# Four attentions of a two-block fp32 kernel: the maximum of a group of heads is taken ahead of the scaling of the group before

## What is computed

```python
logits = einsum(q_i, k_t) * scale + d_i - d_k        # first block, causal
p = softmax(where(mask, logits, MASK_VALUE)); o = einsum(p, v_t)

p = softmax(einsum(qb, k)); o = einsum(p, v)         # second block, "A" (axial) and "C" (latent)
p = softmax(sc); p = p[:, :, 0] - lam * p[:, :, 1]   # second block, "B" (differential)
```

## Time and profile before

| what | us |
|---|---|
| median of 3 runs (2878.01 to 2881.4) | 2878.91 |
| the profiled execution, its own time | 2877.92 |
| its span, first to last instruction | 2876.1 |
| PE busy / PE weight loads | 2621.8 / 2333.3 |
| DVE busy / ACT busy | 1857.5 / 1528.5 |
| mean granted TensorE clock, share of full | 0.947 |

### The profile page before, as it was taken

The page is one execution under the profiler, slowest core; times in us unless marked ns, Lnnn a source line. Parts: engine busy times, 40 slices in busy tenths (PEclk is TensorE's granted clock), DMA queues, the critical chain, the costliest instruction groups (busy, mean ns, idle before and its releaser), DMA issues.

```text
span 2876.1 us, 38647 instructions
## 1 busy us (share of the span) xinstructions
PE 2621.8 (91%) x16826; PEld 2333.3 (81%) x16826; DVE 1857.5 (65%) x1580; ACT 1528.5 (53%) x1466; POOL 0.2 (0%) x4
## 2 busy tenths in 40 slices
PE   6879999887999999999999997978799989878998
PEld 6769998776787877878787786877689988768998
DVE  5645445564688888888888884454565554546554
ACT  5244434432677767777776774455344444644443
POOL 0000000000000000000000000000000000000000
PEclk9879999987999999999999998999899999889999
DMA  5214554221599999989999894323145533223452
GB/s 202 90 58 147 183 185 158 100 79 59 193 366 349 365 350 361 354 348 362 348 365 351 349 364 158 118 88 132 54 152 191 189 134 118 82 95 114 151 191 88
DMA packets 83099, 585.32 MB, mean 204 GB/s; under 512 B 9480, under 2 KB 11208, under 8 KB 12272
## 3 DMA queue, kind: packets, MB, share of 16 engines
q1 hardware_dynamic: 82928, 582.81, 54.2%
HBM read 581.73 MB, written 1.05 MB: 203 GB/s over the span
## 4 chain that ended last, share of the span: by engine, by line
PE 82%; DVE 10%; ACT 6%; issue 1%; DMA 0%; ACTq 0%; SPq 0%; DVEq 0%
PE PS L1370 80%; ACT whi L500 2%; DVE wlo L842 2%; ACT pb L563 2%; PE PS L1754 1%; ACT pt L579 1%; PE PS L1516 1%; DVE hT L859 1%; DVE stat L937 1%; DVE pb L945 1%; DVE small L855 1%; DVE hT L910 0%; DVE pb L931 0%; DVE qe L1003 0%; DVE ke L1002 0%
## 5 line engine op out<-in xcount | busy, mean ns | idle before, releaser
L842 DVE TENSOR_TENSOR wlo<-raw,whi 128x2048 fp32r<-128x2048 f32 x550 | 1259.5, 2291 | 567.2 <-ACT whi L500 557.1
L500 ACT ACTIVATE whi<-raw 128x2048 fp32r<-128x2048 f32 x550 | 1052.0, 1913 | 375.4 <-PE PS L1370 375.3
L1370 PE MATMUL PS<-hhi,whi 128*128 128x256 f32 x1952 | 573.1, 294 | 31.9 <-DVE hlo L865 19.0
L1370 PE MATMUL PS<-hlo,whi 128*128 128x256 f32 x1952 | 563.9, 289 | 0.0
L1370 PE MATMUL PS<-hhi,wlo 128*128 128x256 f32 x1952 | 562.9, 288 | 0.0
L1370 PEld LDWEIGHTS PS<-hhi,whi 128*128 128x128 f32 x1952 | 385.7, 198 | 46.5 <-issue 40.6
L1370 PEld LDWEIGHTS PS<-hlo,whi 128*128 128x128 f32 x1952 | 386.6, 198 | 0.6 <-issue 0.5
L1370 PEld LDWEIGHTS PS<-hhi,wlo 128*128 128x128 f32 x1952 | 385.7, 198 | 0.0
L1370 PE MATMUL PS<-whi,xghi 128*128 128x512 f32 x896 | 360.0, 402 | 2.1 <-ACT pm L667 2.1
L1370 PE MATMUL PS<-whi,xglo 128*128 128x512 f32 x896 | 355.2, 396 | 0.0
L1370 PE MATMUL PS<-wlo,xghi 128*128 128x512 f32 x896 | 355.0, 396 | 0.0
(11 more groups left out here) (331 smaller groups left out, 3757.3 us busy)
## 6 DMA issues: line engine op xcount, KB each, us to landing
raw<-in_wm SPq DMA_DIRECT2D x336, 1024.0 KB, 5.0
raw<-in_ws SPq DMA_DIRECT2D x214, 1024.0 KB, 4.8
xT<-in_xT SPq DMA_DIRECT2D x1, 1024.0 KB, 4.9
bsum<-in_bsum SPq DMA_DIRECT2D x1, 1024.0 KB
out_T<-hT SPq DMA_DIRECT2D x4, 256.0 KB, 2.5
lmask<-in_lmask SPq DMA_DIRECT2D x1, 512.0 KB
tri<-in_tri SPq DMA_DIRECT2D x1, 256.0 KB
cmask<-in_cmask SPq DMA_DIRECT2D x1, 256.0 KB
```

Source lines behind the costliest of these rows:

```text
L500: act.activation(whi[s % SPLIT][:], raw[s % RAW][:], ACT.Copy).then_inc(hi_ready, 1)
L842: dve.tensor_tensor(wlo[s % SPLIT][:], raw[s % RAW][:], whi[s % SPLIT][:].bitcast(F32), ALU.subtract).then_inc(lo_ready, 1)
L1370: return pe.matmul(out, a, b, start=start, stop=stop, skip_group_check=True)
```

## The change

In each of the three `attention` functions the index of the later steps moves by one, and the loop runs one n longer. On DVE the scaling of group n-1 now follows the maximum of group n; the transpose is of group n-2 and the value product of group n-3. No buffer, bank, instruction or size changes. Because the loops run one n longer, `fill()` is called once more in axial (n = 0 to 6) and once more in diff (n = 0, 2, ..., 10).

```diff
@@ ACT attention @@
-                for n in range(len(jobs) + 2):
+                for n in range(len(jobs) + 3):
...
-                    if n >= 2 and jobs[n - 2].value:
+                    if n >= 3 and jobs[n - 3].value:
                         after(mixed)
-                        act.activation(jobs[n - 2].dst, PS[:, 6, 0:2 * P].rearrange("p (t q) -> p t q", t=2),
+                        act.activation(jobs[n - 3].dst, PS[:, 6, 0:2 * P].rearrange("p (t q) -> p t q", t=2),
                                        ACT.Copy).then_inc(mixed_out, 1)
                         C.next(mixed_out)
                     if n % fill_every == 0:
                         fill()
-                    if 1 <= n <= len(jobs) and jobs[n - 1].value:
-                        kb = jobs[n - 1].keys // P
+                    if 2 <= n <= len(jobs) + 1 and jobs[n - 2].value:
+                        kb = jobs[n - 2].keys // P
@@ DVE attention @@
-                for n in range(len(jobs) + 2):
+                for n in range(len(jobs) + 3):
...
                     if n % fill_every == 0:
                         fill()
-                    if n < len(jobs):
+                    if 1 <= n <= len(jobs):
+                        j, pb = jobs[n - 1], pbs[(n - 1) % PB]
+                        z = stat[:, (n - 1) % PB, 4:8]
                         after(exped)
                         step(dve.reciprocal(z, z))
                         for i in range(4):
-                            ins = dve.tensor_scalar(pb[:, i, 0:w], pb[:, i, 0:w], z[:, i:i + 1], None, ALU.mult)
+                            w = slice(0, j.keys)
+                            ins = dve.tensor_scalar(pb[:, i, w], pb[:, i, w], z[:, i:i + 1], None, ALU.mult)
                         if j.less is not None:
                             step(ins)
-                            first = pbs[(n - 1) % PB]
+                            first = pbs[(n - 2) % PB]
@@ PE attention @@
-                for n in range(len(jobs) + 2):
+                for n in range(len(jobs) + 3):
...
-                    if n >= 2 and jobs[n - 2].value:
-                        j, pt = jobs[n - 2], pts[weighs % 2]
+                    if n >= 3 and jobs[n - 3].value:
+                        j, pt = jobs[n - 3], pts[weighs % 2]
...
                     if n % fill_every == 0:
                         fill()
-                    if 1 <= n <= len(jobs) and jobs[n - 1].value:
-                        j = jobs[n - 1]
-                        buf = pbs[(n - 1 - (j.less is not None)) % PB]
+                    if 2 <= n <= len(jobs) + 1 and jobs[n - 2].value:
+                        j = jobs[n - 2]
+                        buf = pbs[(n - 2 - (j.less is not None)) % PB]
                         tp = banks(4, 2).rearrange("p (h b q) -> p h b q", h=4, b=NT)
                         claim(4, 2)
-                        pe.wait_ge(probs_ready, before + n)
+                        pe.wait_ge(probs_ready, before + n - 1)
```

More of the change, by code:

```diff
@@ L923, in attention @@
                         sp = PS[:, b:b + 2, :].rearrange("p b (h k) -> p b h k", h=2)
-                        m, z = stat[:, n % PB, 0:4], stat[:, n % PB, 4:8]
+                        m = stat[:, n % PB, 0:4]
                         after(scored)
```

## The result

The changed kernel takes **2906.42 us** (median of 4 runs, 2902.21 to 2907.58) against 2880.15 for the kernel before on the same chips (4 runs, 2878.01 to 2881.54): a ratio of 1.009, 95% interval 1.0076 to 1.0105. It is slower. The forecast was 2900.7, its range 2881 to 2914.

A forecast was written before the change was run, and what follows sets the result against it. PE was taken to bound axial, while waits stand in diff. Terms of 1.1 + 0.7 + 0.8 + 7.5 + 1.8 - 1.0 = 10.9 per layer, twice 21.8, gave 2900.7 us; span 2888 to 2912, 8-in-10 range 2881 to 2914.

The forecast's parts named there:

- Lost cover: cc's head norm loses both filler units that covered its chain: +7.5 us per layer, bounds 6.0 and 9.
- bank 7: Diff's extra filler is followed directly by the head norm's, so PE waits for the bank's emptying: +0.8 us per layer.
- Axial: PE-bound, nothing to gain; three uncovered pt copy waits instead of two: +1.1 us per layer, bounds 0 and 2.4.
- Diff: Shorter pair loop against a first odd scaling delayed behind the split: +0.7 us per layer, bounds -6 and +6.5.
- Fox: Tail gets one more group (5.3), last exp no longer waits 3.50: +1.8 us per layer, bounds 0 and 3.6.
- Latent: No fillers; earlier maxima against a longer tail: -1.0 us per layer, bounds -2.0 and +1.4.
- The sum: All terms together: 10.9 us per layer, twice 21.8, giving 2900.7 us with the median's 1.0.
- The rival that had it faster: Diff's long waits vanish, each saving 7.7 us with its slow unit, 30.8 in all: 2868.5 us; chance 0.12.
- The rival of the clock: Waits move into diff's transposes and slow four units per layer, 2.1 us each, 17 in all: 2917; chance 0.10.
- The signs: No unit in cc's norm, 8 to 10 us to spread; three axial waits; diff waits before transposes; latent maxima 4 apart.

The follow-up runs named there:

- fillers alone: Against the kernel before, pipeline depth unchanged, one more filler call in axial (n=6) and one in diff (n=10): 2899.02 us, ratio 1.0067.
- Depth alone: Against the kernel before, the new depth in all attentions, but no filler in the extra n of axial and diff: 2880.87 us, ratio 1.0003.
- both orders mended: Against the kernel before: diff and latent deeper, no extra fillers; in diff scaling ahead of the weight split, pt copy ahead of the odd exp: 2839.6 us, ratio 0.986.
- the reorderings: Against the kernel before: all deeper, no extra fillers, scaling ahead of split in fox, axial, diff, pt copy ahead of exp at diff's odd n: 2840.01 us, ratio 0.9865.
- DVE's order alone: Against the kernel before: all attentions deeper, no extra fillers, scaling ahead of the weight split in fox, axial and diff, pt copy behind exp: 2874.09 us, ratio 0.9977.

## Why the prediction held, point by point

**Lost cover** (7.5, and 0.8 for bank 7, per layer): right, and the largest term as said. The head norms lost 9.6 and 8.8, with the chain from squares to spread at 1997.33 - 1988.40 = 8.9 us. The choice near fox's bare norm, rather than the full-clock 6.0, is what the sums of 4.42 us bear out. Removing the two fillers brings 2906.4 down to 2880.9. Of these, bank 7 has the 0.78 us of the row at 1972.19 (in layer 1 at 2537.02), as charged; the lost cover alone is then 8.8 and 8.0. With fillers alone axial has two such waits instead of one and pays 6.8 for a unit of 6.0; in the changed kernel it has one as before, and the prediction rightly charged nothing there. A slip that changed nothing: 17 instructions in 6.56 us make 3.9 us for ten, not 4.1. Ten sums took 4.42 and, in layer 1, 3.94.

**Axial** (+1.1): size and make-up are right, +1.1 in both layers, from three waits of 1.21 us instead of two beside the same wait for bank 7. Depth alone cost only 0.3: there too are three waits, but in that kernel no two units follow each other behind axial, and the 0.78 us of bank 7 fall away.

**Diff** (+0.7): the sign is right and the size was too small: the depth costs 3.7 and 3.9, inside the bounds of -6 and +6.5. The delay of the first odd scaling behind the split came, 5.58 us in front of the transpose, though the first value product is only 2.7 late. The step that failed is the length of a pair: 13.1 us were forecast, down from 15, and it stayed at 15.15 or more. The forecast's loop ran over ACT and DVE alone (12.8) with PE's load (10.3) beside it. The rows show them in series: the pt copy stands behind the odd exp on ACT, this exp needs scores that PE makes behind the unit, and the table load of 1.28, which the sum left out, stands between. So the 6 us that three shorter periods were to save did not come, and the delay of 6.5 was 3.8 at the last value product: both were taken too large, and the two errors cancel in part. The clock has a share in this: the forecast kept units at 6.0, and with three long waits instead of two the granted clock of the stage with depth alone is 0.81 instead of 0.85, 1.9 us for the same matmuls.

**Fox** (+1.8): close to the middle of -0.1 and +3.2, but neither layer shows it, so the fit is luck. In layer 0 the last value product ran at full clock (1.09 us), in layer 1 at half (1.98).

**Latent** (-1.0): right in sign and too timid, -3.4. The maxima follow each other by 2.4 to 3.1 us and no longer by 4.5; I had let a longer tail at half clock eat most of the gain, and it did not.

**The sum**: 10.9 per layer was forecast. The five differences of the table, with fox read against 60.0, give 11.0 for layer 0 and 15.5 for layer 1, so 26.5 of a span's 24.2, the rest being the spread of untouched stages. An underrated diff and an underrated latent cancel within the sum, so its closeness is partly luck. By the medians the change cost 26.3 us where 21.8 were forecast. The span of 2888 to 2912 is not what the bounds give: added up they reach from 2876 to 2926.

**The rival that had it faster** priced the long waits of diff at 2 x 7.7 = 15.4 us per layer, units included. With both orders mended diff went from 67.1 and 66.9 to 51.6, so 15.5 and 15.3. Its price was right in sum, though not by parts: waiting before value products fell from 13.0 to 4.0 in layer 0, by 9.0 instead of 11.2, and PE's busy time by 6.4 instead of 4.2. Its condition, that the odd scaling stand ahead of the split, was necessary but not enough: the pt copy had to pass the exp too. The advice of the Trainium skill, Perfetto Trace Analysis, section "Optimization Strategy", to start sooner the dependency that blocks the gap, fits these runs only when every instruction that stands ahead of it in its engine's list is counted: the same earlier maximum in all four attentions gave 1.0003 and, with the reorderings, 0.9865.

**The rival of the clock** (2917) did not come as told: waits of 1.21 us left the clock alone again. The slow unit read above stands behind a wait of 5.58 us.

**The signs.** No unit between squares and spread of cc, three waits in axial and the waits before transposes in diff came as named. The latent maxima are 2.4 to 3.1 us apart rather than the 4 named as a sign, and from the end of y's spread to cc's spread it is 10.3 and 9.8 us, at the edge of the 8 to 10 named.

## What to carry to other kernels

When a software pipeline gets one stage deeper, ask for the moved instruction what stands ahead of it in its engine's list, then for the next one behind it, until the whole round has been walked: here two reorderings that were worth 1.8 to 4.5 us per layer each were worth 19 together. And where a loop consumes filler work from a fixed list, one turn more is not free: it takes cover from a later stage that has none of its own. The best versions keep the filler count, deepen diff and latent, and mend both orders in diff: 2840 us, 1.4% under the kernel before.

## What the hardware showed unexpectedly

- The table load of an exp (1.28 us) sometimes hides in ACT's waiting time and sometimes does not. With DVE's order alone, the load at 2465.90 in the timeline above comes only after ACT has waited 1.78 us for the maximum, and the exp follows it. Some 16 us earlier in the same loop it runs at once, and the exp then waits 0.28 us for its maximum:

```profile
2450.11 1.28 ACT L568 ACT_TABLE_LOAD   x1
2451.67 0.47 ACT L568 ACTIVATE pb<-PS,stat 128x256 f32<-128x256 f32 x1 [0.28 <-DVE stat L943]
```

In the kernel before 14 of the 18 exps with a load have it ahead of the wait; the four others, two in each layer of diff, are those whose exp by the program also waits for a transpose, which frees their probability buffer (PB = 4). In these four the 1.28 us come on top, behind the maximum. That the second wait is the cause is argued from the program; a kernel with more buffers was not run.
- PE at half its clock after idling has a price in neighbours. Ten sums took 4.42 us at a granted 0.51 (layer 0) instead of 2.33 at 1.00, and diff's 404 matmuls took 55.77 busy us at 0.81 and 47.46 at 0.97. So 8.3 of the 19.2 us that mended orders saved in layer 0 are clock rather than waiting.
